# Joined products in three more MLP jobs, and the second norm's row factors by one product with ones

## The reference

```python
h = rms_norm(x, g_mix) * (1.0 + scale1) + shift1
...
x = x + gate1 * mix
h = rms_norm(x, g_mlp) * (1.0 + scale2) + shift2
ff = jnp.square(jax.nn.relu(h @ w_ff1)) @ w_ff2
return x + gate2 * ff
```

## Time and profile before

| what | us |
|---|---|
| median of 3 runs | 1400.32 (1399.94 to 1400.83) |
| the profiled execution | 1399.79 |
| its span, first to last instruction | 1397.5 |
| PE busy | 1376.4 (98% of the span) |
| DVE busy | 848.4 (61%) |
| ACT busy | 586.6 (42%) |
| POOL busy | 477.7 (34%) |

### The profile page before, as it was taken

The page is one execution under the profiler, slowest core; times in us unless marked ns, Lnnn a source line. Parts: engine busy times, 40 slices in busy tenths (PEclk is TensorE's granted clock), DMA queues, the critical chain, the costliest instruction groups (busy, mean ns, idle before and its releaser), DMA issues.

```text
span 1397.5 us, 17631 instructions
## 1 busy us (share of the span) xinstructions
PE 1376.4 (98%) x7050; PEld 1155.7 (83%) x7050; DVE 848.4 (61%) x871; ACT 586.6 (42%) x713; POOL 477.7 (34%) x269
## 2 busy tenths in 40 slices
PE   5999999999999999999999999999999999999998
PEld 4877778898888888888888888888888888888887
DVE  5967688795538974566545564453746434354584
ACT  5667888665325632232222222342322223423252
POOL 0002111145003775574554545531432222332131
PEclk9999999999999999999999999999999999999999
DMA  9444411106311343343433344479997444445552
GB/s 369 170 159 158 152 68 38 46 26 209 128 61 31 118 165 121 132 148 140 155 127 116 126 146 151 163 286 388 387 382 277 151 151 158 171 174 196 199 187 91
DMA packets 75698, 231.25 MB, mean 165 GB/s; under 512 B 5729, under 2 KB 9953, under 8 KB 66786
## 3 DMA queue, kind: packets, MB, share of 16 engines
q1 hardware_dynamic: 75074, 229.60, 44.9%
q10 hardware_dynamic: 544, 0.52, 0.1%
HBM read 165.09 MB, written 65.01 MB: 165 GB/s over the span
## 4 chain that ended last, share of the span: by engine, by line
PE 96%; DVE 2%; DMA 1%; issue 1%; SPq 1%; ACT 0%; POOL 0%; DVEq 0%; ACTq 0%
PE bank L844 17%; PE bank L843 17%; PE bank L845 17%; PE bank L854 10%; PE bank L837 9%; PE bank L838 9%; PE bank L839 9%; PE bank L857 5%; PE bank L889 1%; DMA win_raw<-in_w_in 1%; PE bank L901 0%; DVE two_r L2245 0%; SPq L604 0%; PE bank L910 0%; DVE n_t L2217 0%
## 5 line engine op out<-in xcount | busy, mean ns | idle before, releaser
L2387 DVE TENSOR_TENSOR hin_two<-hin,hin_two 128x3072 fp32r<-128x3072 f32 x28 | 131.4, 4694 | 185.7 <-ACT hin_two L1700 185.7
L2664 POOL TENSOR_TENSOR w_lo<-w_raw,w_hi 128x2048 fp32r<-128x2048 f32 x28 | 134.9, 4817 | 318.8 <-ACT w_hi L1688 317.2
L843 PE MATMUL bank<-hin_two,w_lo 128*128 128x512 f32 (+1 forms) x576 | 211.2, 367 | 0.0
L844 PE MATMUL bank<-hin_two,w_hi 128*128 128x512 f32 (+1 forms) x576 | 210.9, 366 | 0.0
L845 PE MATMUL bank<-hin_two,w_hi 128*128 128x512 f32 (+1 forms) x576 | 210.9, 366 | 0.0
L1688 ACT ACTIVATE w_hi<-w_raw 128x2048 fp32r<-128x2048 f32 x28 | 53.6, 1913 | 247.6 <-PE bank L857 149.5
L2656 POOL TENSOR_TENSOR w_lo<-w_raw,w_hi 128x512 fp32r<-128x512 f32 x43 | 63.3, 1473 | 180.1 <-ACT w_hi L1620 180.0
L845 PEld LDWEIGHTS bank<-hin_two,w_hi 128*128 128x128 f32 x576 | 108.6, 189 | 17.7
L843 PEld LDWEIGHTS bank<-hin_two,w_lo 128*128 128x128 f32 x576 | 108.7, 189 | 17.4 <-issue 0.2
L844 PEld LDWEIGHTS bank<-hin_two,w_hi 128*128 128x128 f32 x576 | 108.6, 189 | 17.4 <-issue 0.2
L2294 DVE TENSOR_TENSOR hid<-bank,hid 128x256 f32<-128x256 f32 x80 | 33.9, 424 | 124.2 <-ACT hid L1636 105.2
(11 more groups left out here) (326 smaller groups left out, 3373.4 us busy)
## 6 DMA issues: line engine op xcount, KB each, us to landing
hin<-hid_all SPq DMA_DIRECT2D x28, 1536.0 KB, 6.7
hid_all<-hid SPq DMA_DIRECT2D x105, 384.0 KB, 2.4
w_raw<-in_w_ff SPq DMA_DIRECT2D x36, 1024.0 KB, 9.0
mod_raw<-in_w_mod SPq DMA_DIRECT2D x16, 1024.0 KB, 6.3
w_raw<-in_w_ff SPq DMA_DIRECT2D x60, 256.0 KB, 3.5
x<-in_xT SPq DMA_DIRECT2D x5, 2048.0 KB, 14.5
w_sums<-w_raw SPq DMA_DIRECT2D x8, 1024.0 KB, 15.5
w_raw<-w_sums SPq DMA_DIRECT2D x8, 1024.0 KB, 9.7
```

The costliest lines, as they stand in the source:

```text
L843: pe.matmul(out, w_lo, v_hi, start=first, stop=False, skip_group_check=True)
L844: pe.matmul(out, w_hi, v_lo, start=False, stop=False, skip_group_check=True)
L2387: dve.tensor_tensor(hin_part(n % 3, LO), hin[n % 3][:].rearrange("p t n -> p (t n)"), hin_part(n % 3, HI), ALU.subtract).then_inc(hin_lo_d ...
L2664: pool.tensor_tensor(w2_lo[n % 2][:].rearrange("p t n -> p (t n)"), w2_raw[m % RAWS][:].rearrange("p t n -> p (t n)"), w2_hi[n % 2][:].rea ...
```

## The change

Three things change. The jobs 2, 3 and 4 are joined as 6 to 15 are (`JOINED`). All three chunks of the second norm get their row factor the way the first did: one product with ones as weights, root and reciprocal over 512 columns in a buffer of the chunk's own in SBUF, no spread. In job 4 the two weight sums for job 5 stand ahead of the last `add_low` and `relu_square`.

```diff
-QH = REST + 2
+JOINED = tuple(q for q in range(2, NJ - 1) if q != REST + 1)
...
-    n_rstd = place("n_rstd", [P, CH], F32, A0 + HALF)
+    n_rstd = [place(f"n_rstd{i}", [P, CH], F32, o) for i, o in enumerate((A0 + HALF, A0 + 2 * HALF + 11 * 2048, A0 + 2 * HALF + 7 * 2048))]
...
-        return len(ADDED) * (q - QH) + ADDED.index(i) + 1
+        return len(ADDED) * JOINED.index(q) + ADDED.index(i) + 1
...
-        return n + 1 if n < NN else n
+        return min(n + 1, NN)
...
                 pe.wait_ge(xn_done, xn_count(n))
-            if n == NN:
+            if n >= NN:
                 pe.matmul(norm_bank(n)[:], ones[:], n_acc[:], start=True, stop=True).then_inc(norm_mm, 1)
...
                 if i == 1 and d == 0:
                     pe.wait_ge(out_evac, KD)
                     norm_sum(NN)
-                elif i == 2 and d == 0:
-                    norm_spread(NN + 1)
...
                 after(pe, ff1_copy, 4 * q)
-                if q > QH:
+                if q - 1 in JOINED:
                     pe.wait_ge(ff1_added, added(q - 1, P4))
...
                 pe.wait_ge(ff1_copy, 4 * q + {P6: 1, P7: 2, P4: 3}[i])
-                if QH <= q < NJ - 1:
+                if q in JOINED:
                     pe.wait_ge(ff1_added, added(q, {P6: P1, P7: P6, P4: P7}[i]))
...
-                if part == 1 and QH <= q < NJ - 1:
+                if part == 1 and q in JOINED:
                     m = grouped(ps[:, buf + CH:buf + 2 * CH],
...
                 ff1_product(q, i)
                 if q == 0 and i == P5:
                     norm_sum(2 * NN - 1)
-                elif q == 0 and i == P6:
-                    norm_spread(2 * NN - 1)
...
-            if n == NN:
-                act.activation(n_rstd[:], norm_bank(n)[:], ACT.Sqrt, bias=eps[:], scale=1.0 / D).then_inc(sd_done, 1)
+            if n >= NN:
+                act.activation(n_rstd[n - NN][:], norm_bank(n)[:], ACT.Sqrt, bias=eps[:], scale=1.0 / D).then_inc(sd_done, 1)
                 return
...
-            if i == P4 and QH <= q < NJ - 1:
+            if i == P4 and q in JOINED:
                 act.activation(hid[j][:, CH:HTOK], ps[:, buf + CH:buf + HTOK], ACT.Copy)
                 act.activation(hid[j][:, 0:CH], ps[:, buf:buf + CH], ACT.Relu).then_inc(ff1_copy, 1)
...
-            if n == NN:
-                dve.reciprocal(n_rstd[:], n_rstd[:]).then_inc(rc_done, 1)
+            if n >= NN:
+                dve.reciprocal(n_rstd[n - NN][:], n_rstd[n - NN][:]).then_inc(rc_done, 1)
                 return
...
             c = chunk_of(n)
             s = SEQ_OF[c]
-            if n == NN:
+            if n >= NN:
                 dve.wait_ge(rc_done, n + 1)
             else:
                 dve.wait_ge(norm_bc, spread_count(n))
-            scale = n_rstd if n == NN else norm_bank(n)
+            scale = n_rstd[n - NN]
...
-            if QH <= q < NJ - 1 and step in (U2, C11, C22, C12, T4):
+            if q in JOINED and step in (U2, C11, C22, C12, T4):
                 dve.wait_ge(ff1_added, added(q, {U2: P5, C11: P2, C22: A_P5, C12: P3, T4: SQ_P4}[step]))
...
         for q in range(1, NJ):
-            low = {U2: (P1, P6, P5), C11: (P2,), C22: (P7, A_P5), C12: (P3,)} if QH <= q < NJ - 1 else {}
+            low = {U2: (P1, P6, P5), C11: (P2,), C22: (P7, A_P5), C12: (P3,)} if q in JOINED else {}
             for step in (U2, C11, B11, C22, B22, C12, B12, T1, T3, T2):
                 if step == C22 and q == NJ - 1:
                     hin_split_lo(0)
                 for i in low.get(step, ()):
                     add_low(q, i)
                 hid_out(q, step)
-            if QH <= q < NJ - 1:
-                add_low(q, P4)
-                relu_square(q)
             if q == REST:
                 w1_add(q + 1, P7)
                 w1_add(q + 1, P3)
+            if q in JOINED:
+                add_low(q, P4)
+                relu_square(q)
             hid_out(q, T4)
```

More of the change, by code:

```diff
@@ L1833, in _ @@
             scale_small(d)
-        act.wait_ge(norm_bc, 2 * NN + 2)
+        act.wait_ge(norm_bc, 2 * NN)
         act.activation(fin_s[:], bank[3][:, 0:QC], ACT.Copy).then_inc(small_r, 1)
@@ L2451, in fin_rstd @@
             dve.wait_ge(sd_done, 2 * NN + h + 1)
-            after(dve, norm_bc, (2 * NN - 1 + h) * h)
+            after(dve, norm_bc, (2 * NN - 3 + h) * h)
             dve.reciprocal(rc_half[:], sd_half[:]).then_inc(rstd_done, 1)
@@ L2462, in final_first @@
         def final_first(tiles):
-            dve.wait_ge(norm_bc, 2 * NN)
+            dve.wait_ge(norm_bc, 2 * NN - 2)
             final(tiles, 0, HTOK, ps[:, 6 * CH:6 * CH + HTOK])
@@ L2472, in final_small @@
         def final_small():
-            dve.wait_ge(norm_bc, 2 * NN + 1)
+            dve.wait_ge(norm_bc, 2 * NN - 1)
             r = bank[7][:, 0:QC].unsqueeze(1).to_broadcast([P, 2, QC])
```

## The result

| | before | changed |
|---|---|---|
| median of 6 runs, us | 1400.21 (1399.94 to 1400.83) | 1409.07 (1407.71 to 1411.73) |
| the profiled execution | 1399.79 | 1410.6 |
| its span | 1397.5 | 1408.7 |

The changed kernel is slower: ratio 1.0066, 95% interval 1.0056 to 1.0077, +8.9 us by the medians.

A forecast was written before the change was run, and what follows sets the result against it. PE, with 96% of the chain, was taken as the bound; DVE's delay in job 0 gave +5.7 us (PE's 1.84 included), joining -0.8: +4.9 on 1399.79, 1404.7, by medians 1405.2; range 1400.8 to 1408.5.

The forecast's parts named there:

- PE's work: Projection and jobs 2 to 4: two chunks save 0.92 us each, three joined jobs 0.82, together 2.66.
- The second chunk's reciprocal, zero: DVE, some 40 us ahead of the projection's end: the longer reciprocal, 3.35 us for 0.17, was taken to cost nothing.
- The walk through job 0: DVE's rows in job 0: long reciprocal, held-up `norm_apply` and POOL turns start job 1 at 480.95, not 475.27: +5.7 us.
- a turn behind POOL: DVE late in job 0: each of POOL's three remaining rows costs DVE about 1.25 us, 3.75 together.
- The clock: Rival: PE idle before job 1 brings the lower clock, 2.2 us taken, half a bound of 4.3; 1407.4 us, chance 0.26.
- one long gap, 475.6 to 480.95: Before job 1: PE idle after 12 matmuls of P4, waiting for C11, about 5 us.
- The joint of jobs 4, 5 and 6: Forecast for jobs 4 and 5: the reordered DVE rows cost zero; the 0.4 us wait may change by -0.4 to +0.4.
- DVE's eight small adds and its squaring per job cost nothing here.: Joined jobs 2 to 4: no cost, since jobs 6 to 15 already have them and PE has no wait there.
- The sign on which I had set the blame for job 4: A new PE wait for job 5's weights longer than 0.8 us would make joining job 4 the culprit.

The follow-up runs named there:

- second_only: The kernel before with only the second chunk's row factor by one product with ones: 1399.03 us, ratio 0.9994.
- third_psum: The kernel before with only the third chunk's row factor by one product with ones, its reciprocal written to PSUM and read there: 1401.68 us, ratio 1.0012.
- third_filled_less: The kernel before with the third chunk by ones (factor in SBUF), plus 10 idle products ahead of job 0's P4, 20 ahead of job 1's P1: 1406.96 us.
- joins_only: The kernel before with jobs 2 to 4 joined and job 5's weight sums first, norms as before: 1403.95 us, ratio 1.003.
- change_store_later: The changed kernel with SP's store of job 4's squared result moved behind the loads of job 6's weights: 1405.41 us, ratio 1.0039.
- join_job2: The kernel before with job 2 alone joined beside 6 to 15: 1401.1 us, ratio 1.0009.

## Why the prediction was wrong

It said 1405.2, at most 1408.5, and slower; slower held, the size did not. By its steps, on the profiled executions:

- **PE's work.** The second chunk gave 0.86 by the medians (0.92 forecast), jobs 2 to 4 gave 0.79 in the changed kernel (0.82). Right.
- **The second chunk's reciprocal, zero.** Right (`second_only`).
- **The walk through job 0.** Job 1 was to start at 480.95 and starts at 480.99, but part of this is luck. Job 0 started 0.9 later than the walk had it, and the walk was 0.9 too long: it gave 28.0 us from the start of job 0 (452.92), and the job takes 27.15. Most of that is a turn behind POOL, 1.25 forecast and 1.0 measured (1.77 less 0.74), three times. The mechanism held: `third_psum`, with the same reciprocal, is 3.9 us shorter in job 0. The rule of the Trainium skill, page "SBUF — State Buffer", section "Who interferes with whom", holds here in kind: 1.77 beside POOL with two SBUF inputs, 0.73 beside POOL with one. A turn cost less than the whole row of the other engine that the rule gives, 1.0 against 1.3.
- **The clock**, put aside as a rival with 0.26. This is the first step that failed. I looked for one long gap, 475.6 to 480.95, and didn't ask what the 2.6 us before P4 would do. The clock fell during that wait, P4 ran at half pace until 476.8, and PE stood idle for another 2.8 us before job 1. These are 2.8 and not the 5.3 of the forecast because P4 at half pace filled some 1.5 of them and the walk was 0.9 too long. Job 1 lost 2.8 us (`third_filled_less` gives them back), near the 2.2 of the rival. That 2.2 came from the pace of eight products at 16.39; the granted clock that the trace gives there (13.40 to 20.20) is 1.00, so that row shows the slower pace, but not the lower level that I read from it. With the forecast's own waits the fallen clock should have been the main case: forecast plus rival was 1407.4. The Trainium skill, page "TensorE: Matmul & The Clock Gate", section "HAM oscillation — how this bites in real kernels", says that idle gaps bring the lower clock back. In kind the trace agrees, at waits of 2.6, 2.8 and 1.8 us; but the page speaks of longer gaps than these, and `joins_only` kept the full clock through 3.3 us in its profiled execution. Here the measurements decide.
- **The joint of jobs 4, 5 and 6, "I take zero".** The second step that failed, +1.9 us and the clock behind it, +1.6; 3.7 by the medians of `change_store_later`. I followed DVE's order to PE, but the squaring that moved behind the weight sums is also what SP's store waits for, and on SP the loads for job 6 are queued behind the store. I had noted the new place of the squaring, and not asked which queue waits for it.
- **"DVE's eight small adds and its squaring per job cost nothing here."** Wrong for job 2: +1.0 where it stands alone (`join_job2`). The comparison with jobs 10 to 12 took jobs in which DVE has slack for one in which it has none. In the changed kernel the slow job 1 covers it.

On the forecast of +4.9 the failed terms are +2.8, +1.9 and +1.6, together +6.3, which makes the 11.2 of the spans. The shorter walk and the later start cancel; that start is an accident of the changed execution, which is 0.9 us late already at the first chunk's product with ones (370.43; 369.50 before). The parts don't add by the medians: -0.9, +8.2 and +4.0, run alone, make 11.3, and the change measures 8.9, since the slow job 1 covers job 2's wait of 1.0, the loads landed 1.5 us sooner in the changed execution than in that of `joins_only`, and the clock's price varies.

The sign on which I had set the blame for job 4 ("a new wait of PE for job 5's weights longer than 0.8") was set on the wrong job: the wait is for job 6's.

## What to carry to other kernels

Before an operand of a DVE row moves from PSUM to SBUF, see whether the row has another input in SBUF and whether POOL works beside it. Here the move made four rows wait about 1.0 us each, which is more than all the matmuls that the change saves (forecast with 2.7 us). When an instruction moves behind others on its engine, list everyone who waits for its semaphore, the DMA queue too, and then what is queued behind that waiter. And once a forecast has PE waiting several times for a few microseconds in a row, put the lower clock behind the waits into the sum, not beside it.

## What was not expected of the hardware

- **The clock doesn't go by the longest wait.** It fell amid waits of 2.6 and 2.8 us with P4 between them, and after a single one of 1.8 us at 612.5. It stayed full after waits of 1.5 and 1.3 us (`third_psum`) and after a single one of 3.3 us (`joins_only`, in the profiled execution; three others of its seven have a mean clock of 0.997 or 0.998). What decides between these was not found.
- **DVE and POOL take turns row by row.** Neither lost more than one row of the other: POOL's three rows at 472.82, 474.76 and 476.61 took 1.98, 1.72 and 1.57 us, and DVE's three beside them 1.76, 1.76 and 1.78. An application loses 1.0 us, less than the 1.3 that a POOL row takes alone.
- **The reciprocal costs the same with its result in PSUM**, 3.35 us for 512 columns as in the earlier trace rows, so the place of the result was free to choose here.
- **Loads of the same size land at different times.** The 256 KB blocks of `w_raw` for job 6 took 4.2 us (median) in the changed kernel, 5.7 in `joins_only`, 6.5 in `third_filled_less` and 5.0 in the kernel before. Whether PE waits at job 6, and how long, hangs on that as much as on the time of issue.
